# Linear attention of a two-network kernel: masked weights by predicated copies, split gates, states computed earlier, a readout by heads, and query, key and value projections in three reduced-precision products

## What is computed

```python
def gla_rule(q, k, v, gk, state):
    c = GLA_CHUNK
    tri = jnp.tril(jnp.ones((c, c), dtype=bool))[:, :, None]
    def step(s, xs):
        qc, kc, vc, gc = xs
        bcum = jnp.cumsum(gc, axis=-2)
        rel = jnp.exp(jnp.where(tri, bcum[..., :, None, :] - bcum[..., None, :, :], -jnp.inf))
        a_qk = jnp.einsum('bhid,bhjd,bhijd->bhij', qc, kc, rel)
        o = (jnp.einsum('bhij,bhjv->bhiv', a_qk, vc)
             + jnp.einsum('bhid,bhdv->bhiv', qc * jnp.exp(bcum), s))
        last = bcum[..., -1:, :]
        s = (s * jnp.exp(last[..., 0, :])[..., None]
             + jnp.einsum('bhjd,bhjv->bhdv', kc * jnp.exp(last - bcum), vc))
        return s, o
```

## Time and profile before

| | |
|---|---|
| median of 3 runs | 2920.62 us (2920.09 to 2921.76) |
| profiled execution | 2921.71 us |
| its span | 2919.7 us |
| mean granted clock of the matrix engine | 0.975 of full speed |
| instructions | 43409 |
| PE busy | 2746.5 us (94%) |
| DVE busy | 1635.2 us (56%) |
| ACT busy | 1147.5 us (39%) |
| POOL busy | 375.6 us (13%) |

### The profile page before, as it was taken

The page is one execution under the profiler, slowest core; times in us unless marked ns, Lnnn a source line. Parts: engine busy times, 40 slices in busy tenths (PEclk is TensorE's granted clock), DMA queues, the critical chain, the costliest instruction groups (busy, mean ns, idle before and its releaser), DMA issues.

```text
span 2919.7 us, 43409 instructions
## 1 busy us (share of the span) xinstructions
PE 2746.5 (94%) x16596; PEld 2251.1 (77%) x16596; DVE 1635.2 (56%) x2739; ACT 1147.5 (39%) x2093; POOL 375.6 (13%) x583
## 2 busy tenths in 40 slices
PE   6999899999898997999899999998999998997899
PEld 4646777777747996887688888877777786975899
DVE  4455533334655657885377777773433344378665
ACT  4233422222434445346345455543322234332443
POOL 0000000000000000000176666630000000042000
PEclk9999999999999998999999999999999999998999
DMA  7253244442363543223200000032444423200453
GB/s 280 83 211 154 98 173 172 173 162 87 107 240 132 186 179 139 92 96 112 91 1 1 2 1 1 2 130 87 155 174 172 182 94 126 87 30 15 152 181 143
DMA packets 49612, 343.33 MB, mean 118 GB/s; under 512 B 5296, under 2 KB 7344, under 8 KB 9776
## 3 DMA queue, kind: packets, MB, share of 16 engines
q1 hardware_dynamic: 44960, 324.03, 30.1%
q10 hardware_dynamic: 4496, 17.15, 1.5%
HBM read 333.82 MB, written 7.34 MB: 117 GB/s over the span
## 4 chain that ended last, share of the span: by engine, by line
PE 87%; DVE 6%; ACT 4%; issue 2%; DMA 1%; POOL 0%; DVEq 0%; PEldq 0%; ACTq 0%; PEld 0%; SPq 0%; POOLq 0%
PE ps L540 20%; PE ps L542 19%; PE ps L541 19%; PE ps L1939 4%; PE ps L1926 3%; PE ps L708 3%; PE ps L1918 2%; PE ps L1947 2%; PE ps L763 1%; DMA ring<-in_w_dram 1%; PE ps L568 1%; DVE ring_rest L528 1%; ACT H L514 1%; PE ps L738 1%; PE ps L1881 1%
## 5 line engine op out<-in xcount | busy, mean ns | idle before, releaser
L540 PE MATMUL ps<-hidden_high,w_high 128*128 128x256 f32 (+1 forms) x1160 | 388.4, 335 | 9.8 <-DVE h_rest L536 7.1
L1054 ACT ACTIVATE w_high<-ring 128x2048 fp32r<-128x2048 f32 x124 | 236.9, 1911 | 383.9 <-DMA ring<-in_w_dram 259.3
L540 PE MATMUL ps<-h_high,w_high 128*128 128x512 f32 (+1 forms) x1024 | 351.8, 344 | 16.1 <-DVE h_low L1460 13.6
L541 PE MATMUL ps<-h_low,w_high 128*128 128x512 f32 (+1 forms) x1024 | 347.6, 339 | 0.0
L541 PE MATMUL ps<-hidden_low,w_high 128*128 128x512 f32 (+1 forms) x1024 | 343.5, 335 | 0.0
L1469 DVE TENSOR_TENSOR mix_high<-ring,w_high 128x2048 fp32r<-128x2048 f32 x56 | 128.4, 2292 | 247.3 <-ACT w_high L1054 247.3
L542 PE MATMUL ps<-hidden_high,ring_rest 128*128 128x256 f32 (+1 forms) x872 | 263.7, 302 | 0.0
L2260 POOL TENSOR_SCALAR RS<-C,arena 128x128 f32<-128x128 f32 x128 | 74.9, 604 | 1444.5 <-DVEq L1841 1444.5
L540 PEld LDWEIGHTS ps<-hidden_high,w_high 128*128 128x128 f32 x1160 | 218.6, 188 | 42.9 <-issue 16.6
L540 PEld LDWEIGHTS ps<-h_high,w_high 128*128 128x128 f32 x1024 | 195.8, 191 | 45.1 <-issue 24.8
L1469 DVE TENSOR_TENSOR ring_rest<-ring,w_high 128x2048 fp32r<-128x2048 f32 x68 | 155.9, 2293 | 121.9 <-ACT w_high L1054 121.9
(11 more groups left out here) (404 smaller groups left out, 6015.2 us busy)
## 6 DMA issues: line engine op xcount, KB each, us to landing
ring<-in_w_dram SPq DMA_DIRECT2D x302, 1024.0 KB, 4.9
z_spill<-arena ACTq DMA_DIRECT2D x16, 256.0 KB, 2.0
arena<-z_spill SPq DMA_DIRECT2D x2, 2048.0 KB, 9.4
C<-in_first_dram ACTq DMA_DIRECT2D x1, 2432.0 KB, 10.8
X<-in_x_dram ACTq DMA_DIRECT2D x1, 2048.0 KB, 13.1
x_spill<-X ACTq DMA_DIRECT2D x1, 2048.0 KB, 6.3
X<-x_spill SPq DMA_DIRECT2D x1, 2048.0 KB, 8.2
C<-in_third_dram ACTq DMA_DIRECT2D x1, 2048.0 KB, 8.8
```

The source lines that it names most:

```text
L540: ins = nc.tensor.matmul(out_, w_high, high, start=first, stop=False)
L541: nc.tensor.matmul(out_, w_high, rest, start=False, stop=False)
L1054: nc.scalar.activation(W_HIGH[:, (j + 1) % 2, :], ring[:, s], ACT.Copy).then_inc(sems["w_high"], 1)
```

## The change

1. **Up stage.** All 48 products become triples of F32R products. The query weights of slab 0 and the query tiles are split at the end of the input stage (`dve_low`, after tile 5), the rest in the up stage (`weights(1)`, `weights(2)`). The eight rotary copies move behind the query heads.
2. **First slab of a stage.** `act_w_high` of slab 0 moves ahead of the barrier's waits in `act_mod`, `act_final` and `act_norm` (four stages begin so).
3. **Table.** An `unread` square root of one column stands in `act_mod` and at the head of `act_squares`.
4. **GLA input stage.** The z tiles take banks 2 to 5 only; state sums follow z tiles 0, 1, 3 and 4, state adds z tiles 2, 3, 5 and 6. The tables are copied to F32R (`EXPS`), the gate logs split (the first at slab 8, the others in units 1 to 3), and the first `exp_sums` precedes the barrier.
5. **Exponent sums.** Two fp32 products become four of F32R: high and rest of the logs with the high tables.
6. **Weights.** Multiplies and reduction become eight predicated copies of 128x128, from PSUM, one after the other onto one zeroed tile (four tiles `ATG` now). Each waits for the one before it. The result is the sum wherever each entry is picked by one block.
7. **Readout.** No `gread`, no barriers. A Square with an accumulated sum per unit on ACT (`lengths`), roots in three pieces; DVE writes a diagonal matrix of the inverse root (`DG`); PE multiplies each head's output by it in fp32 in place of a transpose; gate, split and rest go head by head. `act_w_high(0)` and `dve_w_rest(0)` of the output stage stand in the scan's end.

```diff
 def pe_up:
-                pe_slab_gemm(pe, v, j, s, {"cols": 512, ...}, 3, lambda k: PX[:, PQ + k, :], T, 4 * j)
+                    begun, ins = three_products(ps[:, h, 0:T], low_high(k)[:, 0:T], low_rest(k)[:, 0:T], up_high(j, a, a + P), RING_REST[:, s, a:a + P], k == 0, k == 2)
...
 def dve_up:
-            for h in range(HEADS):
-                nc.vector.tensor_copy(KT[64:96, h, :], PX[64:96, PKR, :])
+            weights(1, 1536)
+            for k in (3, 4):
+                dve.wait_ge(sems["h_high"], v.of("h_high", k - 2))
+                dve_low_rest(dve, k, T2)
             for h in range(HEADS):
+                if h == 4:
+                    weights(2, SLAB)
...
+            for h in range(HEADS):
+                nc.vector.tensor_copy(KT[64:96, h, :], PX[64:96, PKR, :])
...
+        def dve_low(dve, v, l):
+            dve.wait_ge(sems["w_high"], v.of("w_high", IN_SLABS + 1))
+            nc.vector.tensor_tensor(RING_REST[:, s, 0:1024]..., ring[:, s, 0:1024]..., UQ01[:].bitcast(F32), ALU.subtract)
+            nc.vector.tensor_tensor(RING_REST[:, s, 1024:1536], ring[:, s, 1024:1536], UQ2[:].bitcast(F32), ALU.subtract).then_inc(sems["w_split"], 1)
+            for k in range(3):
+                dve.wait_ge(sems["h_high"], v.of("h_high", KD + k + 1))
+                dve_low_rest(dve, k, T)
...
 def act_norm:
             act.drain().then_inc(act_stage_end, 1)
+            act_w_high(act, v, W_HIGH if uses is U_NEXT else IN_W, 0)
             act.wait_ge(pe_stage_end, v.stages)
...
 exponent sums:
-                    nc.tensor.matmul(ps[:, 2 + q, :], gk_of(t, d, h), C[:, at + q * 512:at + (q + 1) * 512], start=True, stop=True).then_inc(sems["exp_sum"], 1)
+                nc.tensor.matmul(ps[:, 2 + q, :], GK_HIGH[i // 4][:, hs], EXPS[:, d * 1024 + q * 512:d * 1024 + (q + 1) * 512], start=True, stop=False)
+            for q in range(2):
+                nc.tensor.matmul(ps[:, 2 + q, :], GK_REST[i // 4][:, hs], EXPS[:, d * 1024 + q * 512:d * 1024 + (q + 1) * 512], start=False, stop=True).then_inc(sems["exp_sum"], 1)
...
 def weights:
-                for q in range(2):
-                    dve.wait_ge(sems["pairs"], 2 * i + q + 1)
-                    nc.vector.tensor_tensor(AP_[:, q * 512:(q + 1) * 512], ps[:, 4 + q, :], masks[:, q * 512:(q + 1) * 512], ALU.mult).then_inc(sems["masked"], 1)
-                nc.vector.tensor_reduce(ATG[:, i % 2, :], AP_.rearrange("p (n t) -> p t n", t=P), AX.X, ALU.add).then_inc(sems["weights"], 1)
+                for n in range(8):
+                    q, c0 = n // 4, n % 4 * P
+                    if n % 4 == 0:
+                        dve.wait_ge(sems["pairs"], 2 * i + q + 1)
+                    if n:
+                        dve.wait_ge(dve_step, v.steps()) if n % 4 else dve.wait_ge(sems["masked"], 2 * i + 1)
+                    ins = nc.vector.copy_predicated(ATG[:, 2 * d + i % 2, :], masks[:, n * P:(n + 1) * P], ps[:, 4 + q, c0:c0 + P])
...
 end of the scan, PE:
+                for f in (2 * h, 2 * h + 1):
+                    at = f % 2 * L + t * P
+                    ins = nc.tensor.matmul(ps[:, HEAD_BANK[h], at:at + P], OG[:, t, f * P:(f + 1) * P], DG[:, 4 * t + h, :], start=True, stop=True)
...
 end of the scan, ACT:
+            roots(4, 4, 4)
+            act.wait_ge(sems["pairs"], 30)
+            act_w_high(act, v, W_HIGH, 0)
+            lengths(14)
+            roots(0, 3, 7)
+            lengths(15)
+            roots(3, 1, 8)
```

More of the change, by code:

```diff
@@ new lines, in pe_state_sums @@
+        def pe_state_sums(pe, s):
+            d, t = gla_state(s)
+            if s == 0:
+                pe.wait_ge(sems["log_done"], 8)
+            if s:
+                pe.wait_ge(sems["tail"], s)
+            nc.tensor.matmul(ps[:, 0, :], cst("after", d * P, d * P + P), GK[:, t, d * 512:(d + 1) * 512], start=True, stop=True).then_inc(sems["after_sum"], 1)
+            if s:
+                pe.wait_ge(sems["tile_decay"], s)
+            if s > 3:
+                pe.wait_ge(*out_taken(4 * s - 14))
+            for h in range(GH):
+                ins = nc.tensor.matmul(ps[:, 6, GV + h:GV + h + 1], gk_of(t, d, h), ones[:, 0:1], start=True, stop=True)
+            ins.then_inc(sems["tile_sum"], 1)
```

492 lines of the change are left out of this document (289 added, 203 removed).

## The result

The changed kernel takes 2905.1 us (median of 5, 2903.9 to 2905.7) against 2921.7 (5 runs): a ratio of 0.9941, 95% interval 0.9930 to 0.9952. It is 17 us faster. The forecast was 2887, 35 us faster, with a range of 2877 to 2911: the time lies in the range, the gain is half of what was forecast.

What follows compares the result with a forecast made beforehand. PE held 87% of the chain, but DVE was taken as the bound in the scan's loop. Seven terms summed to -34.3 us from 2921.7, forecasting 2887 us, range 2877 to 2911.

Steps and rivals of the forecast that it cites:

- A: Layer 0's up stage: 48 fp32 products become triples in reduced precision at 0.23 us each, -8.7 us.
- G: GLA's readout: PE's first output product 5.9 us after the last addition, first two tiles done sooner, -11.5 us.
- PE's clock does not fall: Readout's better case: with squares and roots also in ACT's shadow, the term is -14 to -15 us.
- F: GLA's scan loop: predicated copies at 0.32 us replace masks and reductions on DVE, 75.0 against 81.0 us, -6.0.
- rival 1: Scan loop: a predicated copy costs two cycles a column, 0.5 us; loop 94 us, whole 2907; chance 0.30.
- rival 2: Scan loop: a fixed price per predicated copy, 0.93 us each; loop 144 us, whole 2956, slower; chance 0.06.
- Without masks and reductions 30.2 us remain: Scan loop: DVE's remaining work, 22.1 us plus 8.1 of additions and keys, before the change's additions.
- B: Layer 1's up stage with split products, including a longer input-stage end: between -6 and +1.4, taken as -0.1 us.
- E: GLA's start: state work moves among the z tiles, 23.7 us against 28.5, -4.8 us.
- rival 3: GLA's z tiles: ACT's table loads land on PE's path, term +5.5, whole 2897 us; chance 0.09.
- C: Starts of four stages: the first slab's copy moves ahead of the barrier, -2.1 us.
- D: First network's output stages: two table loads of 1.28 us leave the chain, -1.1 us, bounds -2.6 and +1.4.

Runs made afterwards that it cites:

- pool_behind_dve: The changed kernel, with POOL's multiply of each unit waiting for DVE's multiply of the same unit; 2895.2 us, ratio 0.9901.
- slab_two_early: pool_behind_dve with the up stage's third slab split straight after the second, ahead of the query heads; 2890.8 us, ratio 0.9898.
- masks_as_before: The changed kernel with weights formed by two mask multiplies and one reduction per unit instead of eight predicated copies; 2904.1 us, ratio 0.9935.
- conv_aligned: slab_two_early with the convolution stage's split operands and three small areas behind them 32 bytes higher within the work area; 2887.2 us, ratio 0.9878.
- no_silu_loads: pool_behind_dve with Exp instead of Silu in the z tiles, which makes the readout's gate another function; 2889.7 us, ratio 0.9893.

## Why the gain was half of what was forecast

**A and G held.** A: -8.2 measured, -8.7 forecast. The trace's 0.23 us for a product was the right measure; the -10.5 by passes would have been too much. G: PE's first output product comes 5.5 us after the last addition, 5.9 forecast:

```profile
2670.60 0.42 DVE L2968 TENSOR_TENSOR H<-ps,H 128x256 f32<-128x256 f32 x1 [0.36 <-PE ps L2841]
2671.81 2.29 DVE L546 TENSOR_TENSOR ring_rest<-ring,w_high 128x2048 fp32r<-128x2048 f32 x1
2674.41 1.65 DVE L2983 SCALAR_TENSOR_TENSOR arena<-ps,V,arena 128x256 f32<-128x256 f32 x4
...
2676.54 0.36 PE L558 MATMUL ps<-mix_high,w_high 128*128 128x256 f32 x1 [1.28 <-DVE gmix_rest L2989]
```

From the last addition to the end of the first two tiles, the forecast's own measure, 25.5 us became 11.3, which is -14.2 and the sum's "PE's clock does not fall": the readout's window has a granted clock of 1.00, where the earlier trace rows had 0.60, and the two tiles took 5.8 us, not 8.1. The forecast had carried the clock of 0.66 over, though PE now has the head products (28 records in one run, 4 later) right ahead of them. Of the 14.2, 1.5 us are lost again at once, in a step the sum did not have: the second slab's copy on ACT starts at 2679.7, and PE waits for its subtraction. So the account has -12.7.

```profile
PE ps L558 <- DVE ring_rest L546: 1.9, 2, 1.5
```

**F failed, by 6.4 us, the largest part.** The price of the copy was right (0.325 forecast, 0.3375 from start to start), rival 1 (0.5) and rival 2 (0.93) are refuted. The step that failed is "Without masks and reductions 30.2 us remain": it took the 22.1 us of the multiplies as fixed. They are not; their length depends on whether POOL's multiply starts first. The trace of the kernel before told it: 1577 ns in the mean for an operation that takes 1.23 alone, and a POOL instruction of 3.41 us that takes 2.35 in the five units where it is first. In the loop the multiplies went from 22.1 to 25.2 us, the logs' subtractions, forecast at 2.1, to 4.4, and the two of tail keys from 1.4 to 2.1. These 6.1 us are nearly all of the 6.6 by which the loop (81.6) missed its forecast (75.0). In pool_behind_dve the three are 17.1, 2.1 and 1.4, 11.1 us less, and the loop gained 9.7. The forecast of 75.0 us was met, and passed (71.9), once the order was fixed: it had carried over 4.9 us of the lock that the kernel before already had. The prediction had named a sign for F that was missed, DVE's idle time under 5 us: it was 9.0, of which some 4 lie between the chained copies. "Worth nothing while DVE is last", of the exponent sums, was not tested in the changed kernel itself, and is wrong by 4 to 7 us once the order is fixed.

**B failed, by 3.1 us.** The tail of the input stage grew by 1.5 us (21.5 from its last slab's copy to PE's first product of the up stage, against 20.0), 1.4 forecast. The keys' products began 13.9 us after the stage's first product, 13.1 forecast. The parts that the forecast lists for this add up to 11.7 only; the trace's other part is 2.3 us in which DVE waits for ACT's copy before the second slab's subtraction. The step that failed is "With 16.6 for keys and values": they took 19.2 us, since the clock was at 0.50 for the first 4.8 us behind the idle time. The stage lasted 34.0 us to the attention's first product against 32.4 before, where 1.5 less was forecast. In slab_two_early the granted clock stays at 1.00 through these products, and the stage gains 5.2 us.

**E failed, by 3.3 us.** The state work cost 14.5 us among the z tiles (141.0 against 126.5 from the second slab to the last z product), 13.9 forecast, and rival 3 is refuted: its loads cost nothing. The step that failed is the end: 9.8 us forecast behind the z tiles, 12.3 measured. One Exp table load of 1.28 us had been left out, and DVE and POOL, starting at the same time, took 6.7 us for DVE's first two multiplies. The clock was left out too: it is 0.75 in this stretch, and the first unit's 14 pair records took 3.2 us where a loop's take 1.56.

**C and D** gave about -1.7 in layer 0; the stretch with C in the second network gave -2.5, -0.6 forecast, and was not taken apart. D lost 1.6 in layer 1, 0.1 forecast. The preload's place was costed (+1.4) but its gain at the other end (-1.28) was not seen in the whole.

**Not in the sum at all:** +4.8 in stages without an edit, of which 15 slabs of the convolution stage at 0.24 are 3.6, against -1.4 in the first MLP; together 2 to 3 us. And +1.7 in layer 1's input stage, where the granted clock differs over one slab, before (first row) and after:

```profile
750.00:753.00 3.00, 3.00 (x26) 2.91 (x25) 1.04 (x1) 2.22 (x2) 0.00 (x0) 1.00 0.56 167
```

```profile
740.00:743.00 3.00, 3.00 (x17) 3.00 (x16) 0.95 (x1) 1.91 (x1) 0.00 (x0) 0.52 0.53 164
```

PE stood for 2.2 us ahead of it in both kernels. This was not tested. The slab took 9.2 to 9.3 us in nine of the 17 profiles (among them before, masks_as_before, conv_aligned and no_silu_loads) and 10.5 to 10.8 in eight (the changed kernel, pool_behind_dve, slab_two_early and base_at_128 among them). What decides it is open, and it adds 1.5 us of scatter to any comparison of two such profiles.

**The range and the signs.** That 2905 lies in the range is luck: its part above 2897 stood for rival 1, and the copies' 0.30 us refutes rival 1. Neither of the two conditions under which the prediction called itself wrong came true (copies over 0.37 us; A and G below 15, they gave 20.9), though half of the gain was missing: neither looked at the instructions that the change leaves alone.

**The best version** is base_at_128: POOL behind DVE, the third slab split early, and the area placed at a multiple of 128. 2884.7 us, ratio 0.9862 (0.9846 to 0.9879), 1.4% faster than the kernel before and 0.8% faster than the change.

## What to carry to other kernels

Before an engine's busy time is taken as its work, compare one instruction's shortest and mean duration: where they differ, another engine may be in it, and an edit that shifts phases can move it. Where two engines hold each other up, put them in order with one wait: PE then waited 3.4 us for POOL, and the loop still gained 9.7, more than the 5.7 of the eight-instruction rewrite beside it. When a new tile goes ahead of others, look at the addresses behind it, and compare a stage without edits in both traces before explaining the ones with edits.

## What the runs showed of the hardware

- A DVE multiply with two SBUF inputs, started while POOL's runs, takes 2.0 to 3.4 us where it takes 1.23 alone, and ends 1.1 us after POOL's; started first, it takes 1.23 and POOL's takes 3.41 instead of 2.35. DVE instructions with one source in PSUM keep their length (the copies 0.30 us in both kernels).
- A predicated copy of 128 columns from PSUM with an int32 mask takes 0.30 us, 0.34 from start to start in a chain that waits for each. The 1.30 us for 512 columns from SBUF doesn't carry over.
- Products of 512 columns of unchanged form take 226.7, 231.7 or 233.3 ns (11.20 / 48) at the same granted clock, with their high operands at 0, 32 or 64 modulo 128 bytes in SBUF.
